# Two-layer hybrid block (attention mixers and mixtures of experts): the merges at a mixer's end reordered, the last expert pair's output handled in halves, and w_in loaded by column parts

## The reference, cut to what matters

```python
# x: 256 tokens x 1024; two layers, ALPHA = (2 * DEPTH) ** 0.25
for layer in range(2):
    h = _swa_nsa_mixer(x, ...) if layer == 0 else _mla_mixer(x, ...)
    x = _layer_norm(ALPHA * x + h, ln_mix_g[layer], ln_mix_b[layer])
    f = _moe(x, ...)          # 64 experts, 6 per token, D_EXPERT 256, and a shared expert
    x = _layer_norm(ALPHA * x + f, ln_ffn_g[layer], ln_ffn_b[layer])

def _swa_nsa_mixer(x, w_in, ...):      # layer 0
    parts = split(x @ w_in)            # 1024 x 2072: q, k, v of three attention branches, and gates
    ...                                # banded, compressed, selected and windowed attention
    return concat(o_swa, o_nsa) @ w_out

def _mla_mixer(x, ...):                # layer 1: latent attention, 16 heads
    ...
    return o.reshape(B, S, 1024) @ w_out
```

## Time and profile before

| | |
|---|---|
| median of 3 runs | 1278.81 us (1278.33 to 1281.76) |
| profiled execution, its own time | 1280.48 us |
| its span in the trace | 1278.4 us |
| mean granted TensorE clock | 0.982 |
| TensorE matmul busy | 1187.5 us (93%) |
| VectorE, ScalarE busy | 367.8 us (29%), 257.0 us (20%) |
| loaded and stored | 444.55 MB, mean 348 GB/s |

### The profile page before, as it was taken

How to read it: one execution, slowest core, us unless ns; L and a number is a source line. 1 busy time by engine, 2 the same in 40 slices (tenths; PEclk the granted TensorE clock), 3 DMA queues, 4 the chain that set the end, 5 groups by cost and what they waited for, 6 DMA issues and landing times.

```text
span 1278.4 us, 20339 instructions
## 1 busy us (share of the span) xinstructions
PE 1187.5 (93%) x8235; PEld 673.9 (53%) x8235; DVE 367.8 (29%) x746; ACT 257.0 (20%) x546; POOL 16.0 (1%) x22
## 2 busy tenths in 40 slices
PE   7998899999999998989869989999999999999984
PEld 4554465555556554646435645564646655454541
DVE  0575561212122121212142456221212212121213
ACT  1232421111112111111104532211211111111110
POOL 0000000000000000000000000000000000000000
PEclk9998999999999999999979999999999999999997
DMA  9535249999999999999991535799999999999993
GB/s 346 150 130 233 107 199 377 418 419 419 419 419 419 420 421 420 421 420 419 420 387 41 197 149 223 322 418 420 418 419 417 419 420 420 421 420 421 419 420 140
DMA packets 67754, 444.55 MB, mean 348 GB/s; under 512 B 7664, under 2 KB 12144, under 8 KB 16368
## 3 DMA queue, kind: packets, MB, share of 16 engines
q1 hardware_dynamic: 67696, 443.71, 85.1%
HBM read 442.63 MB, written 1.05 MB: 347 GB/s over the span
## 4 chain that ended last, share of the span: by engine, by line
PE 61%; DMA 31%; DVE 3%; issue 2%; ACT 1%; POOL 1%; SPq 0%; POOLq 0%; DVEq 0%
DMA ring<-in_expert_w_up 31%; PE psum L852 22%; PE psum L875 9%; PE psum L971 5%; PE psum L800 3%; PE psum L902 3%; PE psum L692 3%; PE psum L584 2%; PE psum L1112 2%; PE psum L728 2%; PE psum L706 1%; PE psum L637 1%; PE psum L627 1%; PE psum L759 1%; PE psum L886 1%
## 5 line engine op out<-in xcount | busy, mean ns | idle before, releaser
L852 PE MATMUL psum<-ring,arena 128*64 128x256 f32 x4032 | 458.8, 380 | 33.6 <-DMA ring<-in_expert_w_up 21.3
L852 PEld LDWEIGHTS psum<-ring,arena 128*64 128x64 f32 x4032 | 297.7, 137 | 211.7 <-DMA ring<-in_expert_w_up 31.3
L875 PE MATMUL psum<-ring,room 128*64 128x512 f32 x1008 | 233.8, 598 | 1.9 <-issue 1.0
L1808 DVE TENSOR_TENSOR y_low<-psum,y_high 128x1024 fp32r<-128x1024 f32 x64 | 78.4, 1225 | 366.6 <-ACT y_high L1276 366.6
L875 PEld LDWEIGHTS psum<-ring,room 128*64 128x64 f32 x1008 | 69.5, 136 | 133.5 <-issue 112.6
L1799 DVE SCALAR_TENSOR_TENSOR room<-room,arena,psum 128x256 f32<-128x256 f32 x64 | 30.7, 480 | 347.8 <-PE psum L852 347.8
L1276 ACT CAST y_high<-psum 128x1024 fp32r<-128x1024 f32 x64 | 64.8, 1013 | 250.9 <-PE psum L875 250.9
L1290 ACT COPY room<-psum 128x256 f32<-128x256 f32 x64 | 23.9, 373 | 262.9 <-PE psum L886 262.9
L902 PE MATMUL psum<-y_high,spread 32*128 32x512 f32 x512 | 65.5, 501 | 5.0 <-issue 4.9
L800 PE MATMUL psum<-onehot,x_high 128*128 128x256 f32 x256 | 66.0, 298 | 0.0
L800 PE MATMUL psum<-onehot,x_low 128*128 128x256 f32 x256 | 63.0, 283 | 0.0
(11 more groups left out here) (237 smaller groups left out, 875.0 us busy)
## 6 DMA issues: line engine op xcount, KB each, us to landing
ring<-in_expert_w_gate SPq DMA_DIRECT2D x126, 1024.0 KB, 18.7
ring<-in_expert_w_up SPq DMA_DIRECT2D x126, 1024.0 KB, 19.7
ring<-in_expert_w_down SPq DMA_DIRECT2D x126, 1024.0 KB, 18.0
ring<-in_swa_nsa_w_in SPq DMA_DIRECT2D x8, 1036.0 KB, 14.0
room<-in_swa_nsa_w_out SPq DMA_DIRECT2D x2, 2048.0 KB, 7.9
room<-in_mla_w_out SPq DMA_DIRECT2D x1, 4096.0 KB, 23.2
ring<-in_mla_w_in SPq DMA_DIRECT2D x1, 2688.0 KB, 19.7
ring<-in_mla_w_uq SPq DMA_DIRECT2D x1, 2304.0 KB, 12.5
```

The lines of the kernel that those rows point to most:

```text
L852: mm = pe.matmul(BANK[2 + m][CAP * e:CAP * e + CAP, 0:DE], xg[:, c, 2 * j + e, :], expert(stored[e])[0][:, c, m, :], start=c == 0, stop=c ...
L875: mm = pe.matmul(PS[0][CAP * e:CAP * e + CAP, half * 512:(half + 1) * 512], ht[:, c, CAP * e:CAP * e + CAP], expert(stored[e])[1][:, c, ha ...
L1808: V.tensor_tensor(ylo, PS[0][:, :], yhi.bitcast(F32), ALU.subtract).then_inc(sem[f"yd_dve{L}"], 1)
```

## The change

Five edits. **(1)** w_in comes as 8 loads of the first 1024 columns and 2 loads of the rest (4 row blocks each), the two counted on `cmpw_in`; `fill` and the gate products wait until all of `cmpw_in` (now 160) is there. The first products start when chunk 0's columns are written and go through one chunk at a time for blocks 0 to 3. **(2)** ScalarE's copy of `cpt` stands ahead of the exponentials of unit 8. **(3)** VectorE adds chunk 0's halves before the attention output of chunk 1 is copied (layer 0), or between the last two units (layer 1), where it also normalises chunk 0 ahead of the copy. Chunk 1's sums and norm come before all of `x_low`. **(4)** TensorE makes both halves of chunk 1 before it turns chunk 0; in layer 1 chunk 0's products are spread otherwise, and 8 of chunk 1's 16 come before the last two units' values, into `PS[1]` instead of `PS[3]`. **(5)** The last pair of a layer's experts is handed on by halves: `tail_pe` after the first half of down, two copies of 512 columns, two low parts, and `pe_combine_tail` with 128-row products, 4 to a half; `layer_norm` adds each half as it is ready.

```diff
-        WIN_PARTS = (1, 2, 2, 3)
+        WIN_PARTS = (1, 1, 2, 4)
         def win_part(c):
-            return min((c + 1) // 2, 3)
+            return (0, 1, 2, 2, 3, 3, 3, 3)[c]
...
-                sp.dma_start(win0[:, c, :], w0[:, c, :]).then_inc(sem[f"win_in{win_part(c)}"], 16)
+                sp.dma_start(win0[:, c, 0:D], w0[:, c, 0:D]).then_inc(sem[f"win_in{win_part(c)}"], 16)
+            for half in range(2):
+                rest = slice(half * KC // 2, (half + 1) * KC // 2)
+                sp.dma_start(win0[:, rest, D:IN0], w0[:, rest, D:IN0]).then_inc(sem["cmpw_in"], 16)
...
-            columns_ready(pe, 0, 1)
+            columns_ready(pe, 0, 0)
...
-            for c in range(KC // 2):
-                pe.wait_ge(sem[f"win_in{win_part(c)}"], WIN_PARTS[win_part(c)] * 16)
-                for n in range(2):
-                    for tc in range(TC):
+            for tc in range(TC):
+                columns_ready(pe, 0, tc)
+                for c in range(KC // 2):
+                    pe.wait_ge(sem[f"win_in{win_part(c)}"], WIN_PARTS[win_part(c)] * 16)
+                    for n in range(2):
                         project(n, tc, c)
...
             def fill(a, b):
+                pe.wait_ge(sem["cmpw_in"], 160)
...
             act_turned(act, 0, 6)
-            act_exp(act, 0, 8)
             act.wait_ge(sem["cpt_pe"], 1)
             nc.scalar.copy(cpt, v(BANK[3], u=4, q=P)).then_inc(sem["cpt_act"], 1)
+            act_exp(act, 0, 8)
...
-        OUT = (PS[0], PS[3])
+        OUT = ((PS[0], PS[3]), (PS[0], PS[1]))
...
             n = OUT_STEPS[L]
-            pe_out_part(pe, L, 1, range(n))
+            pe_out_part(pe, L, 1, range(n - 4, n))
+            pe_out_part(pe, L, 1, range(2 * n - 4, 2 * n))
             pe_columns(pe, st, 0, "lnmix_dve", TC * L)
-            pe_out_part(pe, L, 1, range(n, 2 * n))
             pe_logits(pe, L, 0)
...
             pe_scores(pe, 1, 5)
-            pe_out_part(pe, 1, 0, range(3, 6))
+            pe_out_part(pe, 1, 0, range(3, 8))
             pe_turn_probs(pe, 1, 4)
             pe_scores(pe, 1, 6)
+            pe_out_part(pe, 1, 0, range(8, 10))
             pe_values(pe, 1, 4)
-            pe_out_part(pe, 1, 0, range(6, 8))
+            pe_out_part(pe, 1, 0, range(10, 12))
             pe_turn_probs(pe, 1, 5)
             pe_scores(pe, 1, 7)
             pe_values(pe, 1, 5)
-            pe_out_part(pe, 1, 0, range(8, 11))
+            pe_out_part(pe, 1, 0, range(12, 16))
             pe_turn_probs(pe, 1, 6)
+            pe.wait_ge(sem["o_dve"], BOTH["o_dve"] + 3)
+            pe.wait_ge(sem["max_dve"], BOTH["max_dve"] + 2 * 7 + 1)
+            pe_out_part(pe, 1, 1, range(4))
             pe_values(pe, 1, 6)
-            pe_out_part(pe, 1, 0, range(11, 14))
             pe_turn_probs(pe, 1, 7)
-            pe_out_part(pe, 1, 0, range(14, 16))
+            pe_out_part(pe, 1, 1, range(8, 12))
             pe_values(pe, 1, 7)
...
+        def pe_combine_tail(pe, L, p, half):
+            pe.wait_ge(sem["tailhi_act"], 2 * L + half + 1)
+            pe.wait_ge(sem["taillo_dve"], 2 * L + half + 1)
+            pe.wait_ge(sem[f"spread_dve{L}"], p + 1)
+            cols = slice(half * 512, (half + 1) * 512)
+            for tc in range(TC):
+                for part in (yhi, ylo):
+                    mm = pe.matmul(ACC[tc][:, cols], spread[:, 1, tc * P:(tc + 1) * P], part[:, cols],
+                                   start=False, stop=part is ylo)
+                if half or tc == TC - 1:
+                    mm.then_inc(sem["acc_pe"], 1)
...
+            def y_high_tail(p):
+                act.wait_ge(sem[f"comb_pe{L}"], p)
+                act.wait_ge(sem["tail_pe"], L + 1)
+                nc.scalar.copy(yhi[:, 0:512], BANK[0]).then_inc(sem["tailhi_act"], 1)
+                act.wait_ge(sem[f"down_pe{L}"], (p + 1) * 2)
+                nc.scalar.copy(yhi[:, 512:D], BANK[1]).then_inc(sem["tailhi_act"], 1)
...
-                    dve.wait_ge(sem["acc_pe"], L * TC + tc + 1)
-                    r = xrow[:, tc, :]
-                    link(V.scalar_tensor_tensor(r, r, ALPHA, ACC[tc][:, :], ALU.mult, ALU.add))
-                    V.bn_stats(stats[:, 0:6], r[:, 0:512])
-                    link(V.bn_stats(stats[:, 6:12], r[:, 512:1024]))
+                    for half in range(2):
+                        dve.wait_ge(sem["acc_pe"], L * BOTH["acc_pe"] + 1 + (1 + tc) * half)
+                        r = xrow[:, tc, half * 512:(half + 1) * 512]
+                        link(V.scalar_tensor_tensor(r, r, ALPHA, ACC[tc][:, half * 512:(half + 1) * 512], ALU.mult, ALU.add))
+                        link(V.bn_stats(stats[:, 6 * half:6 * half + 6], r))
                     normed(tc, "ffn")
...
+                def y_low_tail():
+                    for half in range(2):
+                        cols = slice(half * 512, (half + 1) * 512)
+                        dve.wait_ge(sem["tailhi_act"], 2 * L + half + 1)
+                        V.tensor_tensor(ylo[:, cols], BANK[half], yhi.bitcast(F32)[:, cols], ALU.subtract)\
+                            .then_inc(sem["taillo_dve"], 1)
...
             normalise(0, UNITS[0][11], 11)
+            summed(0, 0, 0)
+            summed(0, 0, 1)
             nsa_columns(1)
-            mixed(0)
+            first_mixed(0)
+            second_mixed(0)
...
             heads_out(2)
+            summed(1, 0, 0)
             normalise(1, U[7], 7)
+            summed(1, 0, 1)
+            first_mixed(1)
             heads_out(3)
-            mixed(1)
+            second_mixed(1)
```

More of the change, by code:

```diff
@@ L691, in pe_out_part @@
                 half, c = i // n, i % n
-                mm = pe.matmul(OUT[tc][:, half * 512:(half + 1) * 512], attot[L][:, c + KC - n, tc * P:(tc + 1) * P],
+                mm = pe.matmul(OUT[L][tc][:, half * 512:(half + 1) * 512], attot[L][:, c + KC - n, tc * P:(tc + 1) * P],
                                wout[:, c, half * 512:(half + 1) * 512], start=c == 0, stop=c == n - 1)
@@ L878, in pe_down @@
                             mm.then_inc(sem[f"down_pe{L}"], 1)
+                if last and j == GP - 1 and not half:
+                    mm.then_inc(sem["tail_pe"], 1)
         def pe_turn(pe, L, p, gathered):
@@ L887, in pe_turn, with pe_combine @@
             mm.then_inc(sem[f"ht_pe{L}"], 1)
-        def pe_combine(pe, L, p, j, turn, last=False):
+        def pe_combine_tail(pe, L, p, half):
[9 more added lines that the diff above has]
+                    mm.then_inc(sem["acc_pe"], 1)
+        def pe_combine(pe, L, p, j, turn):
             if isinstance(p, int) and p == 0:
@@ L903, in pe_combine @@
                                    part[rows, half * 512:(half + 1) * 512],
-                                   start=isinstance(p, int) and p == 0 and turn == 0 and part is yhi, stop=last and turn == 1 and part is ylo)
-                    if last and turn and part is ylo and q >= 2:
-                        mm.then_inc(sem["acc_pe"], 1)
+                                   start=isinstance(p, int) and p == 0 and turn == 0 and part is yhi, stop=False)
             if turn == 0:
                 mm.then_inc(sem[f"half_pe{L}"], 1)
-            elif not last:
+            else:
                 mm.then_inc(sem[f"comb_pe{L}"], 1)
@@ L937, in pe_experts @@
             n_groups = groups(pe, L, group)
-            for turn in range(2):
-                pe_combine(pe, L, n_groups * GP - 1, 1, turn, True)
+            for half in range(2):
+                pe_combine_tail(pe, L, n_groups * GP - 1, half)
         def pe_mixed(pe, L):
@@ L1018, in _ @@
                 mm.then_inc(sem["kcv_pe"], 1)
-            pe.wait_ge(sem["cmpw_in"], 128)
+            pe.wait_ge(sem["cmpw_in"], 160)
             for i in range(2):
@@ L1303, in group @@
                     turned(p)
-                    y_high(p)
+                    if last and j == GP - 1:
+                        y_high_tail(p)
+                    else:
+                        y_high(p)
             groups(act, L, group)
@@ L1567, in normed, with summed, first_mixed @@
                 mark(V.scalar_tensor_tensor(r, r, root[:, 0:1], lnb, ALU.mult, ALU.add), f"ln{part}_dve")
[L1569 to L1577, removed]
-                        link(V.tensor_tensor(r, r, OUT[tc][:, cols], ALU.add))
-                    link(V.bn_stats(stats[:, 6 * half:6 * half + 6], r))
-                summed(0, 0)
-                summed(0, 1)
+            def summed(L, tc, half):
+                dve.wait_ge(sem["out_pe"], L * BOTH["out_pe"] + tc * 2 + half + 1)
+                cols = slice(half * 512, (half + 1) * 512)
+                r = xrow[:, tc, cols]
+                if L:
+                    link(V.scalar_tensor_tensor(r, r, ALPHA, OUT[L][tc][:, cols], ALU.mult, ALU.add))
+                else:
+                    link(V.tensor_tensor(r, r, OUT[L][tc][:, cols], ALU.add))
+                link(V.bn_stats(stats[:, 6 * half:6 * half + 6], r))
+            def first_mixed(L):
```

(5 more changed lines are left out.)

12 lines of the change are left out of this document (7 added, 5 removed).

## The result

| | us, median (lowest to highest, executions) |
|---|---|
| before | 1278.57 (1278.12 to 1281.76, 4) |
| changed | 1265.45 (1262.70 to 1268.91, 4) |
| ratio | 0.9893, 95% interval 0.9864 to 0.9923 |

The changed kernel is 13.1 us faster; 14.7 were forecast. Its profiled execution is the slowest of the four: 1268.91 us, span 1267.1, against 1280.48 and 1278.4 before.

What follows compares the result with a forecast made beforehand. Loads at 417 to 421 GB/s bound the expert stages; in the mixers loads are not the limit. Terms +2.0 - 3.4 - 4.0 - 3.5 - 5.8 = -14.7 us, from 1278.81 to 1264.1; range 1259.5 to 1270.5, about 0.84.

Steps and rivals of the forecast that it cites:

- Start, +2.0: Kernel start: fill delayed by all cmpw_in loads, with possible clock loss; +2.0 us, between +0.45 and +3.4.
- that 0.83 us is lost again at once: First products: beginning at 9.25 instead of 10.08 gains nothing, as the fill waits for all cmpw_in loads.
- half a fall: Fill's wait at the start: a clock loss of 1.6 us is possible, half of it taken.
- gaps of 0.8 and 1.1 us cost nothing that shows: TensorE's idle gaps: these cost nothing visible, while 2.5 us is followed by products taking 5.29 instead of 3.70 us.
- Copy of cpt, -3.4: Middle of layer 0: unit 9's scores start 1.9 us earlier, clock kept saves 1.5; -3.4 us, between -1.9 and -3.4.
- Mixer 0, -4.0: End of layer 0's mixer: chunk 1's products end 4.9 us earlier, 0.9 lost to `x_low`; -4.0, between -2.5 and -4.5.
- Mixer 1, -3.5: End of layer 1's mixer: waits save 3.4 us, 4.45 with transposes, 0.9 lost; -3.5, between -2 and -4.5.
- The `x_low` part: Mixer ends: chunk 0's `x_low` now stands between last half sum and logits, lengthening that stretch by 0.9 us.
- Tails, -5.8: Ends of both expert stages: handling by halves saves 2.75 us in layer 0, 3.05 in layer 1; between -4.5 and -6.4.
- the stages of experts as long as before: Both expert stages: length fixed by bytes over rate, so the new profile shows them unchanged.
- 512-byte rows: Loads of w_in: by the skill's 512 B rule halved rows cost nothing, making the start's term 0.7 us smaller.
- Rival B: Whole kernel: clock falls at the start, cpt copy and shifted gaps take part back; 1268 to 1273 us, chance 0.18.

Runs made afterwards that it cites:

- start undone: Changed kernel with the edits of the start undone, all else as changed; 1264.00 us, ratio 0.9887.
- its repeat: The changed kernel timed and traced once more, nothing altered; 1265.07 us, ratio 0.9894.
- start alone: Kernel before with w_in by column parts, first products by chunk and the fill's wait on the shared semaphore, nothing else; 1283.45 us, ratio 1.0042.
- tails undone: Changed kernel with the last pair's output and the layer norm as before in both layers; 1269.50 us, ratio 0.9934.
- last tail only: Changed kernel with layer 0's tail of the experts as before the change, layer 1's as changed; 1266.78 us, ratio 0.9900.
- kept busy: Changed kernel with four unread products on TensorE ahead of the fill's wait; 1263.06 and 1261.89 us, ratios 0.9875 and 0.9868.
- second gap busy: Own semaphore kernel plus four unread 256-column products ahead of the wait for the turned compressed keys; 1256.20 us, ratio 0.9829.
- cpt alone: Kernel before with the copy of cpt ahead of unit 8's exponentials, nothing else; 1273.79 us, ratio 0.9959.
- mixers alone: Kernel before with only the edits of the two mixers' ends; 1270.99 us, ratio 0.9942.
- own semaphore: Changed kernel with the rest of w_in on a separate semaphore that the fill waits for; 1261.74 and 1261.82 us, ratios 0.9868 and 0.9849.

## Why the prediction was right, and where it was off

**Start, +2.0 forecast.** This term was mis-sized, and its ground partly wrong. The landing was right: 41.6 where 42.1 was forecast, since the column parts moved at 414 GB/s, not 398. But "that 0.83 us is lost again at once" failed. The first products ended 3.1 us earlier, not 0.8, for two reasons. They came up to pace sooner. Timeline of the weight loads, before:

```profile
14.48 0.34 PEld L971 LDWEIGHTS psum<-ring,room 128*128 128x128 f32 x1 [0.52 <-issue]
15.18 0.19 PEld L971 LDWEIGHTS psum<-ring,room 128*128 128x128 f32 x1 [0.37 <-issue]
```

And changed:

```profile
9.84 0.28 PEld L987 LDWEIGHTS psum<-ring,room 128*128 128x128 f32 x1 [0.52 <-issue]
10.36 0.19 PEld L987 LDWEIGHTS psum<-ring,room 128*128 128x128 f32 x1 [0.24 <-issue]
```

Up to 15 us one came every 0.85 us before; now one comes every 0.43 from 10.4 on. The granted clock stands at 1.00 in both; why the pace was half is not shown. And they no longer wait for whole rows of w_in: its columns for them landed by 16.9 us, all of w_in before by 26.8. Pace alone would have given little, as the kernel with the start undone shows, which was at pace from 13.0 us on and then waited for w_in, to end at 39.5, in an execution that starts 0.6 us earlier (before 40.2, changed 37.1):

```profile
26.40 13.14 PE L984 MATMUL psum<-ring,room 128*128 128x512 f32 x30 [0.32 <-DMA ring<-in_swa_nsa_w_in]
```

With nothing to follow them, those 3 us went into the wait: 3.64 us idle where 1.6 to 1.9 were forecast. The clock fell behind it, as in all five traces with this wait (3.21 to 4.68 us idle), and the forecast had taken half a fall. Its ground for that, that gaps of 0.8 and 1.1 us cost nothing that shows, holds for mixer 1, where waits of 1.34, 0.98 and 1.10 us left the clock at 1.00 (734 to 778 us), but not near 100 us: in the same trace of before the lower clock follows a gap of 1.07 us at 98.15. The length of a gap alone doesn't decide it, and the forecast had no term for that place. Measured at the next set of products: +3.7, +2.9 and +2.0 us in the changed kernel, its repeat, and the start alone, with its range ending at +3.4. The two kernels that differ from the changed one in this wait alone are 2.4 to 3.3 us faster with the clock kept and 3 to 6 without the wait, each with some 2 us of uncertainty and with a stage of experts of another length in the first.

**Copy of cpt, -3.4.** Right in both halves: 3.6, the wait 1.95 and the clock 1.65. What the Trainium skill says in TensorE: Matmul & The Clock Gate, Part 4, of transposes would have kept the second half away. The trace does not agree that it stays away here: transposes stand ahead of the copy (eight instructions, 1.1 us, not the twelve of the forecast), the gap was 0.73 us where 0.8 was forecast, and the clock stayed at 1.00 in the window from 122 to 124. Nothing in these runs shows more than that this gap, behind these instructions, was short enough.

**Mixer 0, -4.0.** 3.75 in the profile; chunk 1's products start 0.5 us later by the schedule as forecast, and from the last half sum to the logits it grew by 0.67 where 0.9 was forecast.

**Mixer 1, -3.5.** 4.5. The products' part was set too small: 5.1 us came off them where 4.45 were forecast. The waits went as forecast (0.86 us is left of 4.2); where the other 0.7 us come from is not shown. The `x_low` part took 0.67, not 0.9. The timed pair of mixers, 7.4, meets the forecast sum of 7.5.

**Tails, -5.8.** 6.0 on their own stretches, 2.75 forecast and 2.9 measured for layer 0, 3.05 and 3.1 for layer 1. The 128-row products, between 0.13 and 0.5 us by forecast, started every 0.23 to 0.34 us and were hidden. But "the stages of experts as long as before" failed: 0.4 (0.1 by the end of the down products) and 1.15 us longer in the profile after, 3.0 in layer 1 in the repeat. Timed, the tails are worth 5.1.

**512-byte rows.** By the rule that the Trainium skill states in DMA: Bandwidth & Descriptors, Specifications, 4.1 KB rows should have moved as fast as 8.3 KB rows. They did nearly: 414 GB/s in the window from 12 to 24 us, 426 before. It spares 0.5 us of the forecast's 0.7. At 512 B itself the trace does not agree: the compression weights moved at 192 GB/s after the change (28 to 38 us), 189 before.

**The sum.** The timed parts, -5.2, -7.4, -5.1 and +5.4, add up to -12.3; the whole gave -13.7 by its ratio. That does not show that the parts don't act on each other: each is known to some 2 us, and with the start's +0.8 in the merge in place of its +5.4 alone the sum would be -16.9. Rival B, the clock taking part of it back, happened at the start in part and near 100 us: in the profile these took 3.3 us more than forecast and the experts 1.25 more, and the other terms, mixer 1 above all, gave 1.15 more; that execution alone, 1268.9, would have been rival B's. In the trace of the repeat the lower clock near 100 cost less (the output products that stand at 116.56 above stand 4.1 us earlier, 1.25 late in place of 5.3) and layer 1's experts took 3.0 us more. The mechanisms of the four gains were right; that the median came within 1.4 us of the forecast, with the start and the experts mis-sized, is partly luck.

## What to carry to other kernels

An engine that finishes early in front of a wait gains nothing and may lose its clock: before shortening work ahead of a load, check that the consumer waits for what it reads and not for everything that counts on one semaphore. Where a wait must stay ahead of a run of products and the trace shows the lower clock behind it, a few products that nobody reads can be cheaper than that clock, 1.5 to 2.9 us at the place each time here. And time each part of a merge in both directions: an edit that costs 5.4 us alone may cost 1 in the merge, and be worth several once its one bad wait is gone.

## What the runs showed of the hardware

Layer 1's stage of experts was long (446.9 to 448.7 us) or short (445.5 to 446.1), by kernel and not by execution. The difference begins with the stage's first loads. In each trace one packet of the instruction queue (0.02 MB) is moved near the moment when the queue issues the first two loads of gates. All fourteen traces; the packet's time is the start of the window of 0.1 us that holds it:

| kernels | packet, us from the first issue | the two issues, us | GB/s, first 10 us | first gate to last up products, us |
|---|---|---|---|---|
| start alone, tails undone, last tail only, kept busy (2), second gap busy | -1.04 to -0.84 | 0.80 | 195 to 204 | 445.5 to 446.1 |
| cpt alone, mixers alone, before | -0.54, -0.44, -0.14 | 0.81, 0.91, 1.20 | 200, 200, 201 | 445.5, 445.6, 445.7 |
| changed (2), start undone, own semaphore (2) | -0.04 to +0.06 | 1.46 to 1.85 | 163 to 188 | 446.9 to 448.7 |

Where packet and issue coincide, the two issues take 1.8 to 2.3 times as long as 0.80 us, and both first loads have landed 8.6 to 9.7 us after the first issue, where the others need 7.2 to 7.3. In four of these five traces TensorE waits 1.85 to 2.80 us at some 930 us for up weights, ahead of a block of products of the shared expert that needs no load; in the fifth, the first of the changed kernel, no such wait stands out. Behind that block the stream of loads has a hole in all five (322 to 392 GB/s in the worst 8 us). The others have 407 and more, but for the second gap busy with 394, whose stage is the longest of the short ones. The kernel with the second gap busy differs from the one with its own semaphore by five instructions of TensorE at 93 us, and the packet came at -0.84 instead of -0.04. That the packet is moved by the place of the instructions, and that it is the cause of the longer stage, is argued from this agreement over fourteen traces; no run moved it by itself. Of the 5.5 us that this kernel has over its neighbour (1256.20 against 1261.74), 1.5 are the clock near 100 us and 1.2 the stage, in the two profiles, of executions that are 2.2 us apart. The rest is probably how long the neighbour's clock falls: its executions spread over 5 us (1258.1 to 1263.4), those of this one over 2.4, and its two traces differ in just that. In one the small products near 94 us took 1.97 us and the early output products 5.38, in the other 3.60 and 6.04, and the router logits of layer 0 stand at 158.40 and 162.02.
